# Split products that stream their moving tile and their accumulator from the last column to the first

## The chip, the cores and the metric

The kernel runs on one core of a Trainium2 chip. The metric is the device time of one execution in microseconds. Of the kernel before, three runs are shown: 2720.47, 2721.14 and 2723.33 us, median 2721.14 us. One further execution was profiled; it took 2719.24 us, and its span from the first to the last instruction is 2717.4 us.

## What is computed

The reference is two transformer blocks, one behind the other, on 256 tokens of width 2048, all in float32. Nearly all of the work is products of the 256 tokens with large weight matrices:

```python
def first_block(x, c, ctx, ...):
    mod_l = silu(c) @ w_ada + b_ada;  mod_c = silu(c_ctx) @ w_ada + b_ada   # w_ada 2048 x 12288
    h_l, h_c = modulate(rms_norm(x), ...), modulate(rms_norm(ctx), ...)
    ... = split(h_l @ w_in), split(h_c @ w_in)        # low-rank q, k and v, rope, convolution gates
    ... attention over 256 + 256 keys, 8 heads; short convolution over tokens ...
    x = x + gt_a * (rms_norm(concat(att, conv)) @ w_out)          # w_out 2048 x 2048
    u = dwconv3(modulate(rms_norm(x)) @ w_up)                     # w_up 2048 x 11008
    a, g = split(u);  x = x + gt_f * ((a * silu(g)) @ w_down)     # w_down 5504 x 2048
    return rms_norm(x)

def second_block(x, ...):
    z = rms_norm(x) @ w_in_2                                      # w_in_2 2048 x 10248
    a = block-sparse attention with a learned choice of blocks, 8 heads
    b = attention with forget gates, 8 heads
    x = x + (sigmoid(g_a) * (a @ w_proj_a_2) + sigmoid(g_b) * (b @ w_proj_b_2)) @ w_out_2
    x = x + square(relu(rms_norm(x) @ w_up_2)) @ w_down_2         # 2048 x 8192, 8192 x 2048
    return rms_norm(x)
```

## The kernel before, in words

The activations lie transposed in the on-chip memory: the 128 partitions hold features, and the free axis holds the T = 256 tokens. A weight matrix streams in once from memory, 512 KB at a time, into one of eight raw slots. TensorE's float32r format keeps fewer bits than float32, so each operand is split in two: ScalarE writes the rounded high part (`whi`, L615), VectorE writes the remainder (`wlo`, L1095), and the activations are kept as a high part in columns 0 to 255 and a low part in columns 256 to 511 of their tile (`h1`, `hctx`, `mix`, `hf`, `hid0`, `hid1`, `h2`, `heads2`, `merged`, `qn`, `kvn`). There are four split slots for the weights.

`block` (L1873) does one 128 x 128 block of weights: three matmuls into the same 256-column accumulator, high x high (L1875), high weights x low activations (L1876), low weights x high activations (L1877). The weights are the stationary operand, with a weight load for each of the three matmuls; the activations are the moving operand. `product` (L1879) is the loop around it: for each of its `nk` tiles of the contraction, and for each of up to four blocks of 128 output features, one call of `block`. One chunk of weights (1024 columns, two tiles of the contraction and four blocks) is 8 blocks, 24 matmuls. The four accumulators of a product lie in two banks of one half of the accumulator memory (`folded(half())`), and products alternate between the two halves: `free` (L1835) waits until the half of two products ago has been read.

What sets the order on TensorE is the order in which its program is written: it waits for the next chunk's low part (`drained`), issues the matmuls, and with the last of them releases the slot (`chunk_used`), for which ScalarE waits ahead of its next rounding. Between products or at set chunks inside them, small work is inserted by hooks: attention steps, sums of squares with a float32 all-ones matrix (L2168), sums of the modulation vector (L1846). `key_values` (L2041) calls `block` too, eight times. Not through `block` go the modulation product of the first 125 us (`rows`, L1988), where the weights are the moving operand with 512 columns, the token products that make values by tokens (`token_product`, L1902, 512 moving columns; the lower half of `key_values`), and the forget logits (L2324 to L2326).

`groups` (L1918) runs pairs of products in a hardware loop; the others are written out.

Of the kernel before, what the change touches and what calls it, by code (L numbers as in the profile page):

```python
# [10 lines left out]
T = 256  # L11
# [176 lines left out]
def program(nc, ins, consts, out, known, traced):  # L188
    with ExitStack() as ctx:
# [1632 lines left out]
        def _(pe):  # L1822
            L = Stream(pe, "pe", known, traced)
            mm = nc.tensor.matmul

            def half(ahead_=0):
                return halves[(L.n.get("half_read", 0) + ahead_) % 2]
# [26 lines left out]
            def chunk(width):  # L1854

                L.add("drained")
                pe.wait_ge(s_drained, L.at("drained"))
                s = L.split_slot()
                return [w[:, s, :] for w in (whi, wlo)]
# [12 lines left out]

            def block(o, b, hi, lo, x, k, nk):  # L1873

                mm(o, hi, x[:, 0:T], start=(k == 0 and b % 2 == 0), stop=False, skip_group_check=True)  # L1875
                mm(o, hi, x[:, T:2 * T], start=False, stop=False, skip_group_check=True)  # L1876
                return mm(o, lo, x[:, 0:T], start=False, stop=(k == nk - 1), skip_group_check=True)  # L1877

            def product(operands, nk=KT, width=GW, blocks=(0, P, 2 * P, 3 * P), ready=None, with_mod=False, sums=0,  # L1879
                        side=None, done=None):  # L1880


                free(len(operands))
                for k, hi, lo, last in tiles(nk, width, ready, sums):
                    if with_mod and k == KT // 2:
                        pe.wait_ge(s_half_read, L.at("half_read"))
                        mod(1)
                    for a, (src, nth) in enumerate(operands):
                        for b, at in enumerate(blocks):
                            ins_ = block(folded(half(nth))[:, b, :], b, hi[:, at:at + P], lo[:, at:at + P], src(k), k, nk)  # L1890
                    if last:
                        ins_.then_inc(s_chunk_used, 1)
                        L.mark("chunk_used", done if k == nk - 1 else None)
                        L.add("hi_ready")
                        for hook in side.get(k // KC, ()) if side else ():
                            next(hook)
                turn(len(operands))
# [147 lines left out]
            def key_values(p):  # L2045
                pe.wait_ge(s_act_lo, L.of("act_lo", ("kvn", 1)))
                free()
                hi, lo = chunk(KC * GW)
                hi, lo = [w.rearrange("p (k n) -> p k n", k=KC) for w in (hi, lo)]
                for k in range(KC):  # L2050
                    for b in range(4):
                        at, x = (b // 2) * 2 * P, kvn[:, k, (b % 2) * 2 * T:(b % 2 + 1) * 2 * T]
                        ins_ = block(folded(half())[:, b, :], b, hi[:, k, at:at + P], lo[:, k, at:at + P], x, k, KC)
                ins_.then_inc(s_projected, 1)
                L.mark("projected", ("k1", p))
                turn()
                free()
                for s in range(4):
                    o = folded(half())[:, s, :].rearrange("p (h n) -> p h n", h=2)
                    for k in range(KC):  # L2060
                        vh, vl = [w[:, k, :].rearrange("p (h a n) -> p h a n", h=2, a=2)[:, :, 1, :] for w in (hi, lo)]
                        base = (s // 2) * 2 * T + (s % 2) * P
                        xh, xl = kvn[:, k, base:base + P], kvn[:, k, base + T:base + T + P]
                        mm(o, xh, vh, start=(k == 0 and s % 2 == 0), stop=False, skip_group_check=True)
                        mm(o, xh, vl, start=False, stop=False, skip_group_check=True)
                        ins_ = mm(o, xl, vh, start=False, stop=(k == KC - 1), skip_group_check=True)
                ins_.then_inc(s_chunk_used, 1)
                L.mark("chunk_used")
                L.add("hi_ready")
                turn()  # L2070
# [241 lines left out]
            for s in range(4):  # L2312
# [5 lines left out]
                if s == 1:  # L2318
                    free()
                    hi, lo = chunk(8)  # L2320
                    o = half()[0:HEADS, 0, 0:T]
# [79 lines left out]
```

## Time and profile before

| | us |
|---|---|
| median of three runs | 2721.14 |
| profiled execution | 2719.24 |
| its span | 2717.4 |
| TensorE busy (matmuls) | 2625.7 |
| TensorE busy (weight loads) | 2541.3 |
| VectorE busy | 1737.9 |
| ScalarE busy | 1223.6 |
| mean granted TensorE clock | 0.986 |

Matmul and weight load are separate rows of TensorE, and they overlap. A matmul's duration in the profile runs from its start to a modelled end, and successive matmuls overlap in it, so the distance from one start to the next says what one costs; a window of known length with its count gives the mean of it. A granted clock of 1.00 is 2.4 GHz, 0.50 is 1.2 GHz. DMA is the mean busy share of the core's 16 DMA engines.

### The profile page before, as it was taken

How to read it: one execution, taken by the hardware profiler on the slowest of the kernel's cores; microseconds unless marked ns; L12 is line 12 of the kernel's file. 1: busy time of each engine (PE TensorE's matmuls, PEld its weight loads, DVE VectorE, ACT ScalarE, POOL GpSimd, SP SyncE). 2: the span in 40 equal slices, each digit the busy share in tenths (PEclk: the TensorE clock that was granted, in tenths of full speed). 3: DMA queues.
4: the chain of work that ended last, by engine and by line, in shares of the span. 5: the costliest groups of instructions: out<-in, count | busy, mean ns of one | idle time of the engine just before them, and what ended most of it. 6: DMA issues, size and time to landing. Idle time of an engine off the chain costs nothing.

```text
span 2717.4 us, 51131 instructions
## 1 busy us (share of the span) xinstructions
PE 2625.7 (97%) x21394; PEld 2541.3 (94%) x21394; DVE 1737.9 (64%) x2021; ACT 1223.6 (45%) x1487; POOL 114.5 (4%) x196
## 2 busy tenths in 40 slices
PE   6899997889999999999999999999999999999998
PEld 4699877789999999999999999999999999999997
DVE  5988777778888755665565555555555555555554
ACT  6743333344454544444543445444444444434433
POOL 0000324300000000000000010000000000000000
PEclk9999999989999999999999999999999999999999
DMA  9877766747777655565655555666556656566662
GB/s 355 280 232 261 251 205 214 247 163 247 249 239 250 205 194 179 161 221 171 192 180 163 171 162 156 195 194 194 186 172 197 193 195 193 194 190 194 195 209 100
DMA packets 289064, 553.56 MB, mean 204 GB/s; under 512 B 19386, under 2 KB 28712, under 8 KB 288232
## 3 DMA queue, kind: packets, MB, share of 16 engines
q1 hardware_dynamic: 288328, 548.53, 62.1%
q8 instruction: 142, 2.33, 0.3%
q10 hardware_dynamic: 544, 2.29, 0.2%
q14 instruction: 50, 0.41, 0.0%
HBM read 548.53 MB, written 2.10 MB: 203 GB/s over the span
## 4 chain that ended last, share of the span: by engine, by line
PE 86%; DVE 8%; ACT 2%; issue 2%; DMA 1%; POOL 1%; SPq 0%; ACTq 0%; DVEq 0%; POOLq 0%
PE half L1875 26%; PE half L1877 26%; PE half L1876 26%; DVE wlo L1095 3%; DMA raw<-in_w_ada 1%; DVE acc L1124 1%; PE half L1909 1%; PE half L1911 1%; ACT whi L615 1%; PE half L1910 1%; PE half L2168 1%; DVE acc L1127 1%; PE half L2245 0%; PE half L1846 0%; PE half L2129 0%
## 5 line engine op out<-in xcount | busy, mean ns | idle before, releaser
L1095 DVE TENSOR_TENSOR wlo<-raw,whi 128x1024 fp32r<-128x1024 f32 (+1 forms) x909 | 1090.7, 1211 | 813.0 <-ACT whi L615 810.7
L615 ACT ACTIVATE whi<-raw 128x1024 fp32r<-128x1024 f32 (+1 forms) x909 | 941.7, 1048 | 1059.9 <-PE half L1877 948.5
L1875 PE MATMUL half<-hf,whi 128*128 128x256 f32 x2400 | 669.4, 279 | 6.5 <-DVE hf L1187 5.2
L1876 PE MATMUL half<-hf,whi 128*128 128x256 f32 x2400 | 668.0, 278 | 0.0
L1877 PE MATMUL half<-hf,wlo 128*128 128x256 f32 x2400 | 667.9, 278 | 0.0
L1875 PE MATMUL half<-hid,whi 128*128 128x256 f32 x1712 | 475.3, 278 | 0.0
L1877 PE MATMUL half<-hid,wlo 128*128 128x256 f32 x1712 | 474.6, 277 | 0.0
L1876 PE MATMUL half<-hid,whi 128*128 128x256 f32 x1712 | 474.6, 277 | 0.0
L1875 PEld LDWEIGHTS half<-hf,whi 128*128 128x128 f32 x2400 | 451.6, 188 | 8.0 <-issue 5.8
L1877 PEld LDWEIGHTS half<-hf,wlo 128*128 128x128 f32 x2400 | 454.1, 189 | 0.0
L1876 PEld LDWEIGHTS half<-hf,whi 128*128 128x128 f32 x2400 | 452.5, 189 | 0.0
L1875 PE MATMUL half<-h,whi 128*128 128x256 f32 x1520 | 429.8, 283 | 5.1 <-issue 3.8
L1876 PE MATMUL half<-h,whi 128*128 128x256 f32 x1520 | 424.2, 279 | 0.0
L1877 PE MATMUL half<-h,wlo 128*128 128x256 f32 x1520 | 424.1, 279 | 0.0
L1877 PEld LDWEIGHTS half<-hid,wlo 128*128 128x128 f32 x1712 | 322.7, 189 | 0.0
L1875 PEld LDWEIGHTS half<-hid,whi 128*128 128x128 f32 x1712 | 321.7, 188 | 0.1
L1876 PEld LDWEIGHTS half<-hid,whi 128*128 128x128 f32 x1712 | 321.6, 188 | 0.1
L1875 PEld LDWEIGHTS half<-h,whi 128*128 128x128 f32 x1520 | 287.7, 189 | 7.2 <-issue 4.6
L1876 PEld LDWEIGHTS half<-h,whi 128*128 128x128 f32 x1520 | 288.1, 190 | 0.6 <-issue 0.2
L1877 PEld LDWEIGHTS half<-h,wlo 128*128 128x128 f32 x1520 | 288.5, 190 | 0.0
L1127 DVE SCALAR_TENSOR_TENSOR acc<-raw,silu_sb,acc 128x512 f32<-128x512 f32 x128 | 96.3, 752 | 4.5
L1124 DVE SCALAR_TENSOR_TENSOR acc<-raw,silu_sb,acc 128x512 f32<-128x512 f32 x112 | 84.3, 753 | 12.0 <-DVE wlo L1095 0.5
(287 smaller groups left out, 3022.7 us busy)
## 6 DMA issues: line engine op xcount, KB each, us to landing
raw<-in_w_up SPq DMA_DIRECT2D x288, 512.0 KB, 4.4
raw<-in_w_in SPq DMA_DIRECT2D x216, 512.0 KB, 3.8
raw<-in_w_down SPq DMA_DIRECT2D x212, 512.0 KB, 4.6
raw<-in_w_ada SPq DMA_DIRECT2D x192, 512.0 KB, 5.2
raw<-in_w_out SPq DMA_DIRECT2D x64, 512.0 KB, 5.0
raw<-in_w_proj_a SPq DMA_DIRECT2D x16, 512.0 KB, 4.5
raw<-in_w_proj_b SPq DMA_DIRECT2D x16, 512.0 KB, 4.3
raw<-in_w_up SPq DMA_DIRECT2D x16, 384.0 KB, 3.3
```

The costliest lines, as they stand in the source:

```text
L615: A(whi[:, s, 0:elems], raw[:, c, 0:elems], ACT.Copy).then_inc(s_hi_ready, 1)
L1095: V.tensor_tensor(wlo[:, s, 0:elems], raw[:, c, 0:elems], whi[:, s, 0:elems].bitcast(F32), ALU.subtract).then_inc(s_drained, 1)
L1124: V.scalar_tensor_tensor(a, w[:, 0, :], s[:, 0:1], a, ALU.mult, ALU.add).then_inc(s_dve_step, 1)
L1127: V.scalar_tensor_tensor(a, w[:, 1, :], s[:, 1:2], a, ALU.mult, ALU.add).then_inc(s_drained, 1)
L1875: mm(o, hi, x[:, 0:T], start=(k == 0 and b % 2 == 0), stop=False, skip_group_check=True)
L1876: mm(o, hi, x[:, T:2 * T], start=False, stop=False, skip_group_check=True)
L1877: return mm(o, lo, x[:, 0:T], start=False, stop=(k == nk - 1), skip_group_check=True)
L1909: mm(o, xh, hi, start=(k == 0), stop=False)
L1910: mm(o, xh, lo, start=False, stop=False)
L1911: ins_ = mm(o, xl, hi, start=False, stop=(k == nk - 1))
L2168: ins_ = mm(sum_bank[:, i * T:(i + 1) * T], ones[:], sq[:, n % 2, b * T:(b + 1) * T], start=(first and i + b == 0), stop=(last and b == 3) ...
```

## The change

In `block` the accumulator and both halves of the moving tile are turned round along the free axis. Column 255 of the moving tile is read first and its sum is written to column 255 of the accumulator; column 0 comes last. The pairing of moving column and output column is as before, so the result of each matmul lies at the same addresses. The stationary operand is not turned. Flags, order and number of instructions are the same.

```diff
             def block(o, b, hi, lo, x, k, nk):
 
-                mm(o, hi, x[:, 0:T], start=(k == 0 and b % 2 == 0), stop=False, skip_group_check=True)
-                mm(o, hi, x[:, T:2 * T], start=False, stop=False, skip_group_check=True)
-                return mm(o, lo, x[:, 0:T], start=False, stop=(k == nk - 1), skip_group_check=True)
+                o, xh, xl = o[:, ::-1], x[:, 0:T][:, ::-1], x[:, T:2 * T][:, ::-1]
+                mm(o, hi, xh, start=(k == 0 and b % 2 == 0), stop=False, skip_group_check=True)
+                mm(o, hi, xl, start=False, stop=False, skip_group_check=True)
+                return mm(o, lo, xh, start=False, stop=(k == nk - 1), skip_group_check=True)
```

All callers of `block` are affected: `product` with every operand, and the first half of `key_values`. The matmuls that don't go through `block` are as before.

## Rows read from the trace of the kernel before

**Rows 1.** The page's parts 1 and 2: busy time, and TensorE in 40 slices.
```profile
PE 2625.7 (97%) x21394; PEld 2541.3 (94%) x21394; DVE 1737.9 (64%) x2021; ACT 1223.6 (45%) x1487; POOL 114.5 (4%) x196
...
PE   6899997889999999999999999999999999999998
```

**Rows 2.** The page's part 4: chain that ended last, shares by line.
```profile
PE half L1875 26%; PE half L1877 26%; PE half L1876 26%; DVE wlo L1095 3%; DMA raw<-in_w_ada 1%; DVE acc L1124 1%; PE half L1909 1%; PE half L1911 1%; ACT whi L615 1%; PE half L1910 1%; PE half L2168 1%; DVE acc L1127 1%; PE half L2245 0%; PE half L1846 0%; PE half L2129 0%
```

**Rows 3.** Groups by line and shape on TensorE: count, busy us, mean ns.
```profile
L1875 PE MATMUL half<-hf,whi 128*128 128x256 f32 x2400 | 669.4, 279 | 6.5 <-DVE hf L1187 5.2 <-DVE wlo L1095 1.2
...
L1875 PE MATMUL half<-hid,whi 128*128 128x256 f32 x1712 | 475.3, 278 | 0.0
...
L1875 PE MATMUL half<-h,whi 128*128 128x256 f32 x1520 | 429.8, 283 | 5.1 <-issue 3.8 <-DVE krope L1308 1.2
...
L1875 PE MATMUL half<-mix,whi 128*128 128x256 f32 x256 | 73.5, 287 | 0.0
L1875 PE MATMUL half<-merged,whi 128*128 128x256 f32 x256 | 71.9, 281 | 0.0
...
L1875 PE MATMUL half<-heads,whi 128*128 128x256 f32 x256 | 70.7, 276 | 0.0
...
L1875 PE MATMUL half<-hctx,whi 128*128 128x256 f32 x48 | 13.9, 289 | 0.0
...
L1875 PE MATMUL half<-qn,whi 128*128 128x256 f32 x48 | 13.6, 282 | 0.0
...
L1875 PE MATMUL half<-kvn,whi 128*128 128x256 f32 x32 | 9.9, 309 | 2.9 <-DVE wlo L1095 2.8
```

**Rows 4.** Windows, TensorE: length, busy us, count, granted clock, DMA share, GB/s.
```profile
0.00:600.00 600.00, 522.96 (x3642) 0.94 0.74 250
600.00:2717.00 2117.00, 2102.69 (x17754) 1.00 0.59 191
```

**Rows 5.** Waits of TensorE from 600 us on: total us, times, longest.
```profile
PE half L2359 <- DVE xt L1161: 2.6, 1, 2.6
PE half L1875 <- DVE wlo L1095: 1.2, 2, 0.9
```

**Rows 6.** Waits of ScalarE from 600 us on, the longest.
```profile
ACT whi L615 <- PE half L1877: 890.1, 553, 3.5
```

**Rows 7.** Windows, TensorE, stretches of product matmuls, and a cold one.
```profile
700.00:790.00 90.00, 90.00 (x768) 1.00 0.73 244
836.00:1149.00 313.00, 313.00 (x2661) 1.00 0.59 194
...
1947.00:2019.00 72.00, 72.00 (x594) 1.00 0.54 174
2020.00:2640.00 620.00, 620.00 (x5473) 1.00 0.62 194
598.00:600.00 2.00, 2.00 (x11) 0.50 0.00 0
```

**Rows 8.** Timeline, TensorE, behind two insertions: start us, duration us, instruction.
```profile
699.16 0.28 PE L1876 MATMUL half<-hf,whi 128*128 128x256 f32 x1
...
700.93 0.28 PE L1876 MATMUL half<-hf,whi 128*128 128x256 f32 x1
...
1354.47 0.28 PE L1876 MATMUL half<-h,whi 128*128 128x256 f32 x1
...
1355.95 0.28 PE L1877 MATMUL half<-h,wlo 128*128 128x256 f32 x1
```

**Rows 9.** Timeline, TensorE, at a granted clock of 0.50.
```profile
597.56 0.41 PE L1877 MATMUL half<-hf,wlo 128*128 128x256 f32 x1
...
599.48 0.41 PE L1877 MATMUL half<-hf,wlo 128*128 128x256 f32 x1
```

**Rows 10.** Timeline, TensorE, 512-column matmuls of a token product.
```profile
1394.62 0.39 PE L1910 MATMUL half<-wlo,h 128*128 128x512 f32 x1
...
1396.45 0.39 PE L1909 MATMUL half<-whi,h 128*128 128x512 f32 x1
```

## The prediction

> **What bounds the kernel now.** I read the page from its first two parts downward. The busy table has TensorE at 97% of a span of 2717.4 us and VectorE at 64%; in the row of forty slices TensorE is at nine tenths nearly everywhere behind the first quarter [rows 1]. The chain that ended last names the three matmul lines of a split product, L1875, L1876 and L1877, with 26% each [rows 2]. These are the lines that the change edits. The groups by line show how much they are: 2400 matmuls of each line read hf, 1712 read hid, 1520 read h [rows 3], and the smaller groups (mix, merged and heads2 256 each, hctx and qn 48 each, kvn 32) bring it to 6528 of each line, 19584 in all. Their mean duration, 278 or 279 ns for hf and hid, isn't what one costs, because matmuls overlap in the records. The price is the distance from one start to the next, so I went to the windows, where a count stands beside a length.
>
> From 600 us to the end TensorE is busy 2102.69 us of 2117 [rows 4], and the waits of that stretch are 2.6 and 1.2 us [rows 5]. The feeders are ahead: the longest repeated wait of ScalarE, 890.1 us in 553 times, is for L1877 of TensorE to release a split slot [rows 6]. So behind 600 us each nanosecond on a product matmul goes straight into the time. Ahead of 600 us TensorE is busy 522.96 us [rows 4], so at most 77 us of anything slower there can hide. The product matmuls ahead of 600 us are 2448 by the loops (816 blocks of three), those behind it 17136.
>
> The distance between starts has two levels at full clock. From 2020 to 2640 us it is 620 us / 5473 = 113.3 ns; from 836 to 1149 us it is 313 us / 2661 = 117.6 ns, both with a granted clock of 1.00 [rows 7]. The level changes at events beside the products: single rows show fifteen distances in 1.77 us (118.0 ns) behind the small sums that end at 699 us, and thirteen in 1.48 us (113.8 ns) behind the square sums that end at 1354 us [rows 8]. With the longest stretches at the upper level laid end to end (700 to 790, 836 to 1149, 1947 to 2019 us [rows 7], and some shorter ones) I put the upper level at a third of all product matmuls, some 6500, and the mean at 114.8 ns. At the low clock level (0.50 granted, 1.2 GHz, from 598 to 600 us [rows 7]) the distance is 213.3 ns: nine distances from 597.56 to 599.48 us [rows 9]. Half of that is 106.7 ns, so at 2.4 GHz a matmul pays 6.6 ns (lower level) or about 11 ns (upper) over its 256 columns. A 512-column matmul of the token product pays more: eight distances in 1.83 us, 228.8 ns each, 15.4 over the 213.3 that twice 106.7 gives [rows 10]. The excess grows with the columns, so it's not a fixed issue cost but something in how operands or sums are supplied, which is where an order of addresses could matter. That is the reason against expecting nothing as a matter of course.
>
> **The change, part by part.** Removed and added instructions: none. Each of the 19584 matmuls stays, with its weight load; its moving pattern starts at column 255 with step minus one and so does its output. Moving element and output column keep their pairing, so every sum lands at the address where it landed before, and evictions, semaphores, slots and DMAs are not touched. Descriptors in the looped parts keep static addresses. No wait is added or moved, and no queue is passed. Weights (whi, wlo) are still loaded in ascending order.
>
> Start and end of a matmul: two successive matmuls of one block write the same accumulator. Ascending or descending, a column is rewritten 256 columns later, one whole matmul, so the distance between dependent additions is the same. Where block b gives way to block b+1 the addresses are disjoint either way. Cost: 0.
>
> Rate within a matmul: the trace of before has no matmul with a descending stream, neither read nor written, so I bound this from both sides. From below: the excess over the bare columns disappears, 13100 x 6.6 + 6500 x 11 = 158 us less, 2561 us. From above: descending streams pass at one column per cycle of the low clock level, 213.3 ns in place of 114.8 [rows 9]: 17136 x 98.5 = 1688 us behind 600 us, 2448 x 98.5 = 241 us ahead of it, of which up to 77 could hide, giving 4571 to 4648 us. In between, the nearest row is the distance that I see at full clock in both levels. I take 0 as the value: in a reversed run the neighbours in time are still the neighbours in memory and each aligned group of neighbouring columns is still used up before the next one is touched. A supply that works in such groups sees as many groups as before. The nearest rows for the price are those of rows 7, and they are what it costs if an order of addresses plays no part.
>
> The Trainium skill speaks against this in "PSUM — Partial Sum Buffer", section Specifications (TRN2): cache lines there have 8 bytes, and any pattern that isn't contiguous slows matmuls significantly. Read strictly, a step of minus one isn't contiguous, and the result would be the third rival below. "Advanced Engine Details and Errata", section PSUM Cachelines, puts it as every two consecutive elements having to be contiguous, which a descending pair still is; by that wording the sum stays at 2721 us, by the strict one it is some 4600 us. No row of before can decide between the two readings.
>
> Around the matmuls nothing else follows: if they keep their rate, ScalarE and VectorE get their releases at the same times. If they were slower, nothing comes late behind them, since the feeders already wait for TensorE [rows 6]; if they were faster by the whole excess, the feeders have 890.1 us of waiting to give, and TensorE stays the bound.
>
> **Sum.** The profiled execution took 2719.24 us, of which 2717.4 are the span; the median of the runs shown is 2721.14 us, 1.9 us above it. 2719.24 + 0 = 2719.24 us, and at the median's level 2721.1 us. I forecast no change.
>
> **The rivals.**
>
> First, the level shifts to the favourable one. The two levels of rows 7 are reached from the same code (hf products run at both), so they look like a relation in time between streams that is set anew at each interruption [rows 8]. A reversed moving stream beside an ascending weight stream changes that relation. If it keeps all at the lower level: 6500 x 4.5 = 29 us less, 2692 us. If it took the whole excess away: 2561 us. For it: the excess grows with the columns. Against it: nothing says which direction is the good one, and two ascending streams that have settled could as well be the best case.
>
> Second, the same mechanism with the other sign. Opposite directions meet again within each matmul where parallel ones can stay clear of each other. If all product matmuls go to the upper level: 13100 x 4.5 = 59 us more, 2780 us. If the excess doubles: 158 us more, 2879 us. Its place is every product matmul, its price 0 to 8 ns of distance, and it decides the sign from 0.28 ns on, because 19584 x 0.28 = 5.4 us is 0.2%. For it: the upper level exists and costs nothing to reach. Against it: at the clock of 0.50 the distance is 213.3 ns with no excess visible, so the supply has reserve.
>
> Third, a reversed pattern isn't taken in pairs and runs at half the column rate: 213.3 ns a matmul, some 4600 us. For it: at full clock the stream passes at twice the rate of the low level, which asks for two columns in the time in which one passes there, and a device that pairs only ascending neighbours would lose just that. Against it: each pair is whole and aligned, only turned round.
>
> A fourth, that the reversal never reaches the chip because both patterns are turned together and the product is the same either way, gives the forecast's own time and needs no price.
>
> **How the numbers follow.** The forecast has 0.45 (the fourth rival within it), a favourable level 0.12 and the loss of the whole excess 0.03, the unfavourable level or a grown excess 0.24, half rate 0.16. A measurement of this kernel tells about 0.2% from no change, 5.4 us. That makes 0.15 for faster, 0.45 for the same and 0.40 for slower. The range goes from 2692 us (all at the lower level) to 2880 us (excess doubled), and leaves half rate and the lost excess out, 0.19 together. The likeliest case's own range is 2716 to 2727 us.
>
> **What would show it.** Right: the instruction counts stay at 21394 matmuls and weight loads; the window from 2020 to 2640 us again has about 5473 matmuls, the one from 836 to 1149 us about 2661, and the mean of the product groups stays at 276 to 279 ns. First or second rival: the counts of both windows move, the clock still at 1.00, and the stretches at either level are longer or shorter, or there is a third level. Third: a distance of some 213 ns at a granted clock of 1.00. The cold stretch at 598 us is the control: if the distance there is above 213.3 ns, a descending stream is limited even at the low clock. The token products (L1909 to L1911) keep their ascending order, so their 228.8 ns must not move; if they do, the cause is not the order of the addresses. The prediction is wrong if the distance of a product matmul moves by over 0.28 ns on the average.

## The result, and the profile after

The changed kernel takes 2770.35 us (median of 4 runs, 2769.04 to 2771.73), against 2722.2 us of the kernel before (4 runs): ratio 1.0179, 95% interval 1.0163 to 1.0196, so it is slower by 48 us. The forecast was no change at 2721.1 us. The time lies in the range, because the range took in the second rival (all product matmuls at the upper distance, 2780 us), and not because the forecast's reasoning allowed it.

The profiled execution took 2769.04 us with a span of 2767.2 us. The page has the same instruction counts as in [rows 1], with TensorE busier by 54 us and the other engines within 3 us of before:

```profile
PE 2680.0 (97%) x21394; PEld 2597.8 (94%) x21394; DVE 1740.1 (63%) x2021; ACT 1223.4 (44%) x1487; POOL 114.3 (4%) x196
```

All line numbers of TensorE below `block` are one higher. The windows of TensorE (length, busy us, count, granted clock, DMA share, GB/s) answer to [rows 7]:

```profile
700.00:790.00 90.00, 90.00 (x767) 1.00 0.75 246
836.00:1149.00 313.00, 313.00 (x2661) 1.00 0.62 194
...
2020.00:2640.00 620.00, 620.00 (x5259) 1.00 0.62 187
```

The stretches that stood at the upper distance have kept their counts to one matmul. The stretch from 2020 to 2640 us, which stood at the lower one, has lost 214 of 5473: 117.9 ns in place of 113.3, at the same clock. At full clock the lower distance is gone. Nearly all of what took its place is the old upper one. Twelve stretches between other work on TensorE hold a third value, 120.0 ns; they are short, 717 matmuls in all, and ten of them lie ahead of 597 us, where the rise is hidden. Seventy distances of one of them take 8.40 us:

```profile
1575.11 0.28 PE L1877 MATMUL half<-h,whi 128*128 128x256 f32 x1
...
1583.51 0.28 PE L1878 MATMUL half<-h,wlo 128*128 128x256 f32 x1
```

The two controls hold. In the cold stretch the distance is again 213.3 ns (nine distances in 1.92 us), and a token product, not turned, has its 94 distances in 21.53 us, 229.0 ns each; in the kernel before the same 94 distances, from 1382.25 to 1403.78 us, take 21.53 us too. The timeline of TensorE in the changed kernel:

```profile
596.78 0.41 PE L1877 MATMUL half<-hf,whi 128*128 128x256 f32 x1
...
598.70 0.41 PE L1877 MATMUL half<-hf,whi 128*128 128x256 f32 x1
```

```profile
1392.38 0.40 PE L1911 MATMUL half<-wlo,h 128*128 128x512 f32 x1
...
1413.91 0.39 PE L1912 MATMUL half<-whi,h 128*128 128x512 f32 x1
```

The first product of the first feed-forward part starts at 596.43 us; in the kernel before it started at 597.00 us. So the rise ahead of it was hidden altogether, and the whole of it lies behind: 2170.8 us from there to the end in place of 2120.4, 50.4 us more. The trace of the kernel before has 2640 product matmuls ahead of this point and 16944 behind it (the prediction had 2448 and 17136), so the rise is 2.97 ns for each. Two thirds of them going up by 4.5 ns is 3.0 ns.

ScalarE's waits for the third matmul of `block`, the answer to [rows 6], have grown by the same 50 us; the feeders only wait longer:

```profile
ACT whi L615 <- PE half L1878: 940.0, 561, 3.5
```

### The profile page after: what moved, and what is told of

Same layout as the page of the kernel before. It is cut to its first block, busy times and chain, and to the rows that moved or that the text cites. A ratio compares the mean times of both kernels' runs of the same rounds, so it can differ in the third digit from the quotient of the medians.

```text
span 2767.2 us, 51131 instructions
## 1 busy us (share of the span) xinstructions
PE 2680.0 (97%) x21394; PEld 2597.8 (94%) x21394; DVE 1740.1 (63%) x2021; ACT 1223.4 (44%) x1487; POOL 114.3 (4%) x196
## 4 chain that ended last, share of the span: by engine, by line
PE 86%; DVE 8%; ACT 2%; issue 2%; DMA 1%; POOL 1%; SPq 0%; ACTq 0%; DVEq 0%; POOLq 0%
PE half L1876 26%; PE half L1878 26%; PE half L1877 26%; DVE wlo L1095 3%; DVE acc L1124 1%; DVE acc L1127 1%; DMA raw<-in_w_ada 1%; PE half L1911 1%; PE half L1912 1%; PE half L1910 1%; PE half L2169 1%; ACT whi L615 1%; PE half L2246 0%; PE half L1846 0%; PE half L2157 0%
## 5 line engine op out<-in xcount | busy, mean ns | idle before, releaser
L1095 DVE TENSOR_TENSOR wlo<-raw,whi 128x1024 fp32r<-128x1024 f32 (+1 forms) x909 | 1092.5, 1212 | 860.4 <-ACT whi L615 858.2
L1878 PE MATMUL half<-hf,wlo 128*128 128x256 f32 x2400 | 677.6, 282 | 0.0
L1876 PE MATMUL half<-hid,whi 128*128 128x256 f32 x1712 | 482.2, 282 | 0.0
L1878 PE MATMUL half<-hid,wlo 128*128 128x256 f32 x1712 | 481.5, 281 | 0.0
L1877 PE MATMUL half<-hid,whi 128*128 128x256 f32 x1712 | 480.1, 280 | 0.0
```

The source lines that it names most:

```text
L1095: V.tensor_tensor(wlo[:, s, 0:elems], raw[:, c, 0:elems], whi[:, s, 0:elems].bitcast(F32), ALU.subtract).then_inc(s_drained, 1)
L1876: mm(o, hi, xh, start=(k == 0 and b % 2 == 0), stop=False, skip_group_check=True)
L1877: mm(o, hi, xl, start=False, stop=False, skip_group_check=True)
L1878: return mm(o, lo, xh, start=False, stop=(k == nk - 1), skip_group_check=True)
```

## The experiments

For each kernel below I give the median and the ratio to the kernel before on the same chip with its 95% interval. The ratio is the recorded one; it can differ by up to 0.0014 from the quotient of the two medians. An interruption is other work on TensorE between two product matmuls, or a pause. What lies between two interruptions is a stretch. A count of levels goes by the starts in the trace: of each stretch of at least 16 matmuls the mean of the fourth to the fifteenth distance is taken. In the kernel before this gives 96 stretches, 45 at the lower distance and 45 at the upper. The kernels e1, e2, f1 and f2 compute something else than the reference and serve for their time alone.

**Which side, and at what grain.** The line of the change that makes `o`, `xh` and `xl` is replaced by the one shown; the three matmuls below it stay.

```diff
 e1: xh, xl = x[:, 0:T][:, ::-1], x[:, T:2 * T][:, ::-1]                    # o as it was
 e2: o, xh, xl = o[:, ::-1], x[:, 0:T], x[:, T:2 * T]
 e5: o, xh, xl = [t.rearrange("p (a b) -> p a b", b=16)[:, ::-1, :] for t in (o, x[:, 0:T], x[:, T:2 * T])]
 e6: the same with [:, :, ::-1]
```

> Only the moving tile is read from the last column to the first; the accumulator is written in ascending order, so the sums of each block lie mirrored (that part of the computation is changed). Theory A (the reads decide: a descending moving stream meets the weight reads in another way and keeps every product matmul at the upper distance): 117.8 ns from start to start everywhere at full clock, about 2770 us. Theory B (the writes decide): the two levels of the kernel before, 113.3 and 117.8 ns, a third at the upper, about 2722 us. Rival C (any disturbance of the start settles the level anew): a mixture that is neither, between 2692 and 2780 us.

Measured: 2773.27 us, ratio 1.0187 (1.0168 to 1.0206), with single runs from 2768.39 to 2783.71; the profiled execution is the slowest of them.

> Only the accumulator is written from the last column to the first; the moving tile is read in ascending order, so the sums lie mirrored (that part of the computation is changed). Theory A (the reads decide): 113.3 and 117.8 ns as in the kernel before, about 2722 us. Theory B (the writes decide): 117.8 ns everywhere, about 2770 us. If each side costs something of its own, both runs with one side turned lie above 2722 us and their rises add up to 48 us.

Measured: 2720.07 us, ratio 0.9997 (0.9983 to 1.0011). Whether the lower distance is lost is decided by the reads; beside ascending reads the order of the writes is free. Windows of the two kernels, reads turned first:

```profile
700.00:790.00 90.00, 90.00 (x753) 1.00 0.72 239
...
2070.00:2640.00 570.00, 570.00 (x4842) 1.00 0.62 186
```

```profile
700.00:790.00 90.00, 90.00 (x767) 1.00 0.73 241
...
2070.00:2640.00 570.00, 570.00 (x5032) 1.00 0.64 195
```

570 us / 4842 is 117.7 ns, 570 / 5032 is 113.3 ns. The first line of the kernel with turned reads shows a third level, 90 us / 753 = 119.5 ns, which no theory had. By the starts it is 120.0 ns, and it holds for 4472 matmuls, where the changed kernel has it for 717. So beside descending reads the order of the writes may matter for which of the two is taken; with one trace of each this is open.

> Read and written alike: groups of 16 columns come in descending order, the columns inside a group in ascending order. The result is that of the reference. If what costs is the coarse direction of the stream (which way it travels through the tile while the weights are read), this is as slow as the changed kernel, 2770 us and 117.8 ns everywhere. If what costs is the step of minus one inside short runs, it's as fast as before, 2722 us with two levels. If a pattern with two dimensions costs by itself, it's above 2770 us.

Measured: 2769.77 us, ratio 1.0184 (1.0167 to 1.0202). In the trace:

```profile
2070.00:2640.00 570.00, 570.00 (x4842) 1.00 0.62 188
```

> Read and written alike: groups of 16 columns come in ascending order, the columns inside a group in descending order. The result is that of the reference. Coarse direction theory: as before, 2722 us with two levels. Step theory: 117.8 ns everywhere, 2770 us. If a pattern with two dimensions costs by itself, this and the run with the groups turned both rise by the same amount.

Measured: 3058.28 us, ratio 1.1243 (1.1223 to 1.1262). None of the theories allowed this. Ascending inside and descending outside gives the changed kernel's time to within 1 us; ascending outside and descending inside costs nearly seven times as much, 313 us / 2354 = 133.0 ns per matmul:

```profile
836.00:1149.00 313.00, 313.00 (x2354) 1.00 0.59 185
```

Transfers by DMA aren't what it meets: the price stands in full where the DMA engines rest. Eighteen distances in 2.40 us are 133.3 ns, in a window with a DMA share of 0.00:

```profile
632.00:637.00 5.00, 5.00 (x40) 1.00 0.00 0
```

```profile
633.53 0.30 PE L1877 MATMUL half<-hf,whi 128*128 128x256 f32 x1
...
635.93 0.30 PE L1877 MATMUL half<-hf,whi 128*128 128x256 f32 x1
```

In e5 and e6 reads and writes are turned alike, and so in all kernels below that turn groups or single matmuls. Only for the whole tile (e1 and e2) are the two told apart; that the reads carry the price of the groups too is argued from there and not shown.

**Are the weight reads the partner?** All 128 columns of the stationary block are read from one:

```diff
+ hi, lo = hi[:, 0:1].to_broadcast([P, P]), lo[:, 0:1].to_broadcast([P, P])
```

> All 128 columns of the stationary block are read from its first column (the weights of a block are replaced by one column, so the products are others); moving tile and accumulator ascending as before. Theory A (moving reads are held up by the weight reads that run beside them): the weight load no longer walks through the memory, so the distance leaves the pair 113.3/117.8 ns and the two levels become one, anywhere from 106.7 to 120 ns. Rival (the moving stream is limited by itself, whatever the weight load reads): the two levels and about 2722 us as before.

Measured: 2708.83 us, ratio 0.996 (0.9945 to 0.9975).

> The same with moving tile and accumulator from the last column to the first. Theory A: the same distance as the run with one column and ascending order, within 0.3 ns, so the same time within 0.3%. Rival (the descending stream is slower by itself): 117.8 ns everywhere and some 48 us above the ascending run.

Measured: 2768.09 us, ratio 1.0175 (1.0158 to 1.0192). Turned, it is 59 us slower than ascending, although the weight load no longer walks anywhere. The windows, ascending first:

```profile
2070.00:2640.00 570.00, 570.00 (x5031) 1.00 0.63 195
```

```profile
2070.00:2640.00 570.00, 570.00 (x4842) 1.00 0.62 188
```

The explanation by two streams that cross falls. That the weight loads play some part isn't excluded, as each matmul still has one beside it; no run left them out. What the addresses of the weight reads do change is which levels an ascending stream falls into, which neither theory had: of 95 stretches the ascending run with one column has 63 at the lower distance, 11 at 117.8 ns and 16 at 120 ns.

**One in three, and larger groups.**

```diff
 f3: as e5 with b=128      g64: b=64      g32: b=32
 f4: only  mm(o[:, ::-1], hi, xl[:, ::-1], start=False, stop=False, ...)  is turned
```

> Read and written alike: columns 128 to 255 first, then 0 to 127, both ascending. The result is that of the reference. If the price hangs on the direction inside the tile (opposite to or along with the weight reads): two levels, 2692 to 2750 us, nearest to 2722. If it hangs on where a matmul starts after the one before it, as the last column read lies beside the first of the next: 117.8 ns everywhere, 2770 us.

Measured: 2719.67 us, ratio 0.9996 (0.998 to 1.0012).

> Only the second matmul of each block (high weights, low part of the activations) is turned, reads and writes alike; the other two ascend. The result is that of the reference. If each turned matmul pays for itself: a third of the rise, 16 us, 2738 us. If the direction of one matmul settles the phase for all: 2770 us with 117.8 ns everywhere. If changes of direction cost too: more than 2770 us.

Measured: 2769.76 us, ratio 1.0179 (1.0162 to 1.0196). One turned matmul in three costs as much as all three. A price for each turned matmul is ruled out at this density. Its window is that of the changed kernel:

```profile
2070.00:2640.00 570.00, 570.00 (x4842) 1.00 0.62 188
```

> Read and written alike: groups of 64 columns come in descending order, ascending inside a group, the result that of the reference. Known: groups of 128 turned leave the time (2720 us), groups of 16 turned give 2770 us. Theory A (any backward jump between neighbouring groups near each other locks the upper distance once it comes often enough): between, at either 2720 or 2770 us and not halfway, because the distance has only levels. Rival (each backward jump has a price of its own): 4 groups in place of 16, a fifth of the rise, 2730 us, with distances that are neither 113.3 nor 117.8 ns.

Measured: 2721.11 us, ratio 0.9997 (0.9978 to 1.0015).

> The same with groups of 32 columns. Theory A: one of the two levels, 2720 or 2770 us. Rival (a price for each jump): 8 groups in place of 16, half of the rise, 2745 us.

Measured: 2767.0 us, ratio 1.0149 (1.0123 to 1.0175). It's one or the other, nothing halfway: four groups of 64 are as before and eight groups of 32 are as the change. With 32 the lower distance is still found in 8 stretches of 94, all of them short and ahead of 597 us. The windows from 2070 to 2640 us, 64 first:

```profile
2070.00:2640.00 570.00, 570.00 (x5032) 1.00 0.63 195
```

```profile
2070.00:2640.00 570.00, 570.00 (x4842) 1.00 0.61 188
```

**Is it the seam between matmuls?**

```diff
- mm(o, hi, xh, start=...); mm(o, hi, xl, ...)
+ mm(o, hi, xl, start=...); mm(o, hi, xh, ...)
```

> All ascending, but the low activations come first in each block: high weights x low, high weights x high, low weights x high. Sums are the reference's, in another order of additions. If the two levels come from which columns follow which from one matmul to the next, their shares move: all at the lower level would be 2692 us, all at the upper 2780 us. If they come from the time at which a stream restarts after an interruption: 2715 to 2730 us as before.

Measured: 2724.07 us, ratio 1.0 (0.9981 to 1.0019). Which tile follows which makes no difference.

**Turning few matmuls.** h1 turns the second matmul of a block only where `k == 0 and b == 0`, i2 where `b == 0`. i1 turns it in the first block behind other work on TensorE, i4 in the third, i3 stands where i1 does but swaps groups of 64.

```diff
+ s = slice(None, None, -1) if k == 0 and b == 0 else slice(None)
+ mm(o[:, s], hi, xl[:, s], start=False, stop=False, skip_group_check=True)
```

> Turned is only one matmul of each product: the second one (high weights, low activations) of the first block at k = 0, reads and writes alike; some 1.6% of all. The result is that of the reference. Theory A1 (a turned matmul puts the streams into the upper phase and they stay there): 117.8 ns nearly everywhere, 2760 to 2770 us. Theory A2 (the lower distance can't be held while descending reads go on, but comes back when they end): two levels, about 2722 us, within 5 us. Rival (each turned matmul sets the phase anew, at random): a share of the upper level near a half, 2715 to 2745 us, with level changes at product starts where there is no interruption.

Measured: 2709.35 us, ratio 0.9941 (0.9922 to 0.9961). This is faster than the kernel before, and below what any of the three theories gave. (The turned matmul is one in some 192, which is 0.5% of all; 1.6% is its share of the second matmuls.) The trace shows how. The stretches at the upper distance still begin at interruptions, but five of them between 676 and 934 us last 11.5 to 11.8 us each, as long as the rest of a product behind a modulation sum (96 matmuls x 0.1178 = 11.3 us). Around the next product's start:

```profile
684.00 0.28 PE L1876 MATMUL half<-hf,whi 128*128 128x256 f32 x1
...
687.54 0.28 PE L1876 MATMUL half<-hf,whi 128*128 128x256 f32 x1
...
688.01 0.28 PE L1878 MATMUL half<-hf,whi 128*128 128x256 f32 x1
...
691.98 0.28 PE L1876 MATMUL half<-hf,whi 128*128 128x256 f32 x1
```

Thirty distances in 3.54 us are 118.0 ns; thirty-five in 3.97 us are 113.4 ns. Nothing stands between them but the turned matmul. It costs nothing visible there. Where a product starts in a stretch that is at the lower distance already, the distances around the turned matmul are some 26 ns longer in all, and the stretch stays at the lower one. In the kernel before, the upper level of 836 us held for 313 us [rows 7]; here that window has 67 matmuls more:

```profile
836.00:1149.00 313.00, 311.83 (x2728) 1.00 0.62 198
...
2020.00:2640.00 620.00, 620.00 (x5466) 1.00 0.63 195
```

> Turned is the second matmul of the first block of each tile of the contraction, one in twelve. The result is that of the reference. If a reset holds for at least twelve matmuls, the distance is 113.3 ns plus the price of one turned matmul over twelve: at no price 2692 us, at 26 ns each (the trace of the run with one per product allows 20 to 30) 2692 + 1632 x 0.026 = 2734 us. If the reset takes longer than twelve matmuls to act, 117.8 ns everywhere and 2770 us.

Measured: 2736.09 us, ratio 1.0056 (1.0037 to 1.0075), against a forecast of 2734. From 2070 to 2640 us:

```profile
2070.00:2640.00 570.00, 570.00 (x4936) 1.00 0.63 192
```

570 us / 4936 is 115.5 ns, 2.2 over 113.3; twelve times that is 26 ns, the price of one turned matmul among ascending ones. It isn't an independent forecast, since the 26 ns came from the trace of h1; what it shows is that the price holds at one in twelve. Where all are descending each pays far less (4.5 ns over the lower distance).

> Turned is the second matmul of the first block that follows other work on TensorE (a hook, a modulation sum, a token product, a key or value step), reads and writes alike; all others ascend. The result is that of the reference. Theory A (a single turned matmul among ascending ones brings the streams from the upper to the lower distance, and the upper one is entered at interruptions): the upper distance goes nearly everywhere, 2692 to 2702 us. Theory A with a condition (it only does so from a settled stream): 2715 to 2725 us. Rival (the gain of the run with one turned matmul per product came from something else than the reset): no change against before, 2722 us.

Measured: 2708.88 us, ratio 0.9963 (0.9945 to 0.9982), with single runs from 2702.01 to 2723.69. This is between what the two forms of the theory gave.

> As the run that turns one matmul behind each interruption, but in the third block behind it, when six matmuls have run ascending. If the reset works on a settled stream only, this is the one that reaches 2692 to 2702 us and the other is not; if it always works, both do.

Measured: 2711.1 us, ratio 0.9952 (0.9932 to 0.9972), single runs from 2700.1 to 2722.2.

> The same places as the run that turns one matmul behind each interruption, but there groups of 64 columns come in descending order, ascending inside, which in all matmuls left the time alone. Theory A (it takes descending reads): two levels, 2715 to 2730 us. Rival (any other order in one matmul resets the streams): as fast as the run with the turned matmul.

Measured: 2725.04 us, ratio 1.0004 (0.9989 to 1.002). It takes a descending read. But the theory that a turned matmul always brings the lower distance is not borne out: both kernels that turn behind interruptions still have runs at 2722 us and over, so in the time a wait for a settled stream makes no difference that can be told either. The profiled execution of the first stays at the upper level from 700 to 790 us (767 matmuls) while it leaves it from 836 us on:

```profile
700.00:790.00 90.00, 90.00 (x767) 1.00 0.73 241
836.00:1149.00 313.00, 311.79 (x2742) 1.00 0.62 200
```

A turned matmul can also do harm. Of the 32 stretches of at least 31 matmuls behind 1400 us, i1 has 11 at the lower distance that were at the upper in the kernel before, and 6 at the upper that were at the lower. j1 below has the same 17. In i4, where the turned matmul comes two blocks later, 11 went down and none up.

**Both places at once, and a repeat.** j2 is h1 once more; j1 turns at both places.

> Turned is the second matmul of the first block behind each interruption and at each product start, all others ascend; the result is that of the reference. If a turned matmul at both places catches more of the stretches at the upper distance than either place alone: 2695 to 2706 us, below the run with one per product (2709). If a turned matmul only sets the streams anew and the level is then drawn as at any interruption, it's within 5 us of the run with one per product.

Measured: 2706.1 us, ratio 0.994 (0.9921 to 0.9959).

> The kernel with one turned matmul per product once more, beside the other on the same chip. If its gain is of the mechanism and not of one chip's draw: 2705 to 2715 us, 0.3 to 0.6% below the kernel before. If it was a draw: within 0.2% of it.

Measured: 2707.54 us, ratio 0.995 (0.9932 to 0.9968). The gain of one turned matmul per product holds on a second occasion; turns behind interruptions add nothing that can be told (1.4 us).

**Where the levels come from.** The expectations speak of levels that are set anew, or drawn, at each interruption. The traces say something narrower. Six profiled executions are of kernels in which no product matmul reads downward column by column: the kernel before, e2, f3, g64, h2 and i3. Behind 1400 us all 32 stretches of at least 31 matmuls have the same level in all six. Between 597 and 1400 us only 3 of 10 have. So the level hangs mostly on the place in the program, and the draw is left to a few long stretches ahead of 1400 us. One of them holds 1212 matmuls from 1155 us on. The kernel before has it at the lower distance and e2 at the upper, while a later one is at the lower in both; the kernel before first:

```profile
1165.00:1290.00 125.00, 125.00 (x1106) 1.00 0.56 190
1700.00:1930.00 230.00, 230.00 (x2032) 1.00 0.61 194
```

```profile
1165.00:1290.00 125.00, 125.00 (x1064) 1.00 0.59 189
1700.00:1930.00 230.00, 230.00 (x2032) 1.00 0.62 193
```

That stretch alone is worth 1212 x 4.5 ns = 5.5 us. The share of the DMA engines doesn't set the level: in [rows 7] the upper one stands at 0.59 and the lower at 0.62.

## Why the prediction was wrong

- **What bounds the kernel**: right. Behind 597 us all of the rise went into the time, and the feeders waited longer for TensorE.
- **The two levels**: right, and the key. That they are set anew at each interruption was only half right: behind 1400 us they go by the place, as the six traces named above show. Over 31 runs of the kernel before, beside one batch, its times go from 2710.45 to 2732.25 us, while the four of the changed kernel stay within 3 us. That fits a few long stretches whose level differs from run to run; the spread was not traced run by run.
- **Start and end of a matmul, writes**: right. Turned writes alone change nothing. The rule "any non-contiguous AP slows matmuls significantly" of the Trainium skill ("PSUM — Partial Sum Buffer", Specifications (TRN2)) doesn't reach a step of minus one: ratio 0.9997. The page that the prediction set against it, "Advanced Engine Details and Errata" of the Trainium skill, section PSUM Cachelines, has the strict sentence too, beside the one on pairs, so the two pages don't differ as the prediction said.
- **Rate within a matmul, cost 0**: this is the step that failed. The term measured 2.97 ns for each of the 16944 matmuls behind 597 us, 50.4 us of span in place of 0. I argued that aligned groups of neighbours are used up whole in either direction, so that their order plays no part. The groups-of-16 runs refute it: used up whole but in descending order they give the changed kernel's time, and turned inside they cost 20 ns a matmul over the lower distance. What the runs show in its place is that descending reads keep the stream from the lower distance. Why they do is open. The Trainium skill ("SBUF — State Buffer", section Specifications (TRN2)) has lines of 16 bytes, with full bandwidth from two hits in a line on. Reversed within 64 bytes each such line still gets four hits in a row, and the run is 12.4% slower; if it is the reads that pay there, which is argued and not shown, two hits in a line aren't enough.
- **Second rival**: its effect was right (all at the upper distance), its reason wrong. It's not the crossing with a weight read that walks the other way, since a stationary operand read from one column keeps the difference at 59 us (that this equals the rival's 59 us is chance). The rival's size was some 10 us too much, mostly because it counted the matmuls ahead of 597 us, whose share is hidden. By the trace they are 2640; two thirds of them at 4.5 ns are 8 us.
- **First rival**: fell for the change, but a few turned matmuls do move the level the good way.
- **Third and fourth rival**: fell. No window of the changed kernel at full clock is near 213 ns, and the counts moved, so the reversal did reach the chip.
- **The chances**: the rival that came true had 0.24 together with its neighbours, and I put 0.45 on no change although I had just found two levels from the same code. With a supply that already pays for its columns, an untried order deserved less trust than half.

Shown: for whole tiles the reads decide; the lower distance is lost when groups of 32 columns or fewer come in descending order (the second matmul of each block, turned, is enough); between groups of 64 and of 32 there is nothing halfway. Not shown: what in the chip holds a stream at its level, why groups of 64 are free, why columns turned inside groups of 16 cost so much more, and why a single turned matmul ends an upper stretch at some places, leaves it at others and starts one at a few.

## What to carry to other kernels

If back-to-back matmuls of one shape run at two distances at full clock, look at the order in which their moving operand is read, before looking for a wait: starts in the timeline, in means over a dozen, show it. For float32r matmuls of 256 columns with a weight load each, keep the moving reads ascending, or in ascending runs of at least 64 columns; with ascending reads the order of writes is free. A single turned matmul at the start of each product gained 0.5 to 0.6% here, twice, but what one does hangs on its place, so it has to be measured. And a kernel with such levels can spread by 0.8% between its fastest and its slowest run (31 runs here), so a single pair of runs can't judge a change of that size.

## What the runs showed of the hardware that was not expected

At full clock the distance of a 256-column float32r matmul held only a few steady values: 113.3, 117.8, 120 and 133.3 ns. Three matmuls together are then 340, 353, 360 and 400 ns, all whole multiples of 6.67 ns, the time of 16 columns at 2.4 GHz (51, 53, 54 and 60 of them, where 48 would carry the columns alone). The 512-column token product fits too: 3 x 229.0 = 687 ns is 103 of them, in both kernels. One descending matmul among ascending ones costs 26 ns, about four such steps. That the chip counts in such steps is read out of these numbers and not tested.
